# Sparse attention in a two-layer trunk: dots in three passes, the indexer's columns first, and the output product by halves of tokens

## What is computed

```python
c_q, c_kv, k_idx, w_idx = jnp.split(h @ w_in, [256, 512, 576], axis=-1)
c_q, c_kv, k_idx = rmsnorm(c_q, q_norm), rmsnorm(c_kv, kv_norm), layernorm(k_idx, kidx_g, kidx_b)
...
    q_idx = (cq_b @ w_qidx).reshape(B, Q_BLOCK, HI, DI)
    dots = jnp.einsum('bthd,bsd->btsh', q_idx, k_idx) * (DI ** -0.5)
    score = jnp.einsum('btsh,bth->bts', jax.nn.relu(dots), w_b).astype(jnp.float32)
    score = jnp.where(causal[None], score, -jnp.inf)
    _, sel = lax.top_k(score, top_k)
    ...
    q = (cq_b @ w_uq).reshape(B, Q_BLOCK, H, dh)
    p = jax.nn.softmax(logits, axis=-1)
...
return out @ w_out
```

## Time and profile before

| | us |
|---|---|
| median of 3 runs | 2018.43 |
| lowest and highest | 2018.05, 2019.6 |
| the profiled execution | 2018.26 |
| its span, first to last instruction | 2016.4 |
| TensorE busy in the span | 1980.2 (98%) |
| VectorE, ScalarE, GpSimd busy | 1346.0, 844.5, 249.7 |
| sparse attention, first to last matmul of its own | 1457.08 to 1656.80 |

### The profile page before, as it was taken

The page is one execution under the profiler, slowest core; times in us unless marked ns, Lnnn a source line. Parts: engine busy times, 40 slices in busy tenths (PEclk is TensorE's granted clock), DMA queues, the critical chain, the costliest instruction groups (busy, mean ns, idle before and its releaser), DMA issues.

```text
span 2016.4 us, 23083 instructions
## 1 busy us (share of the span) xinstructions
PE 1980.2 (98%) x9030; PEld 1618.4 (80%) x9030; DVE 1346.0 (67%) x1673; ACT 844.5 (42%) x1151; POOL 249.7 (12%) x183
## 2 busy tenths in 40 slices
PE   8999999999999999999999999999998899999997
PEld 7788888877877888888888888888875688888886
DVE  7999944443534447999843899983458658999732
ACT  5555632132222224554631555562266535555520
POOL 0000012010010141000021000002224650000031
PEclk9999999999999999999999999999999999999998
DMA  4233123312212232242131333222231013322221
GB/s 168 84 122 129 58 102 112 113 64 100 84 68 85 82 105 84 84 147 104 58 115 64 119 141 110 84 87 100 81 105 42 1 63 142 109 84 98 100 93 65
DMA packets 69719, 189.45 MB, mean 94 GB/s; under 512 B 4016, under 2 KB 12208, under 8 KB 64496
## 3 DMA queue, kind: packets, MB, share of 16 engines
q1 hardware_dynamic: 69376, 187.25, 26.5%
q0 software_dynamic: 240, 0.79, 0.1%
HBM read 185.92 MB, written 2.10 MB: 93 GB/s over the span
## 4 chain that ended last, share of the span: by engine, by line
PE 87%; DVE 6%; issue 3%; ACT 2%; POOL 1%; SPq 0%; DMA 0%; POOLq 0%; DVEq 0%; ACTq 0%
PE bank L1804 13%; PE bank L1806 13%; PE bank L1805 13%; PE bank L1812 12%; PE bank L1814 12%; PE bank L1813 12%; PE bank L1818 2%; PE bank L1820 2%; PE bank L1819 2%; PE bank L2021 2%; PE bank L1911 2%; DVE part_lo L1182 1%; PE bank L2011 1%; PE bank L2130 1%; POOL dsa_temp L712 1%
## 5 line engine op out<-in xcount | busy, mean ns | idle before, releaser
L741 ACT ACTIVATE part_hi<-quad_w 128x1024 fp32r<-128x1024 f32 x280 | 293.2, 1064 | 279.5 <-PE bank L1814 199.8
L1182 DVE TENSOR_TENSOR part_lo<-quad_w,part_hi 128x1024 fp32r<-128x1024 f32 x280 | 330.0, 1217 | 25.7 <-ACT part_hi L741 25.3
L1804 PE MATMUL bank<-gated_hi,out_hi 128*128 128x512 f32 x704 | 274.8, 390 | 0.0
L1806 PE MATMUL bank<-gated_hi,out_lo 128*128 128x512 f32 x704 | 274.1, 389 | 0.0
L1805 PE MATMUL bank<-gated_lo,out_hi 128*128 128x512 f32 x704 | 274.1, 389 | 0.0
L1812 PE MATMUL bank<-part_hi,s_hi 128*128 128x512 f32 x640 | 252.6, 395 | 2.4 <-DVE part_lo L1182 2.4
L1814 PE MATMUL bank<-part_hi,s_lo 128*128 128x512 f32 x640 | 249.6, 390 | 0.0
L1813 PE MATMUL bank<-part_lo,s_hi 128*128 128x512 f32 x640 | 249.2, 389 | 0.0
L1812 PE MATMUL bank<-part_hi,xn_hi 128*128 128x512 f32 x608 | 238.8, 393 | 4.7 <-DVE part_lo L1182 4.7
L1814 PE MATMUL bank<-part_hi,xn_lo 128*128 128x512 f32 x608 | 237.9, 391 | 0.0
L1813 PE MATMUL bank<-part_lo,xn_hi 128*128 128x512 f32 x608 | 237.7, 391 | 0.0
(11 more groups left out here) (207 smaller groups left out, 3385.8 us busy)
## 6 DMA issues: line engine op xcount, KB each, us to landing
quad_w<-w_ffn_in SPq DMA_DIRECT2D x80, 1024.0 KB, 7.3
out_raw<-w_ffn_out SPq DMA_DIRECT2D x64, 704.0 KB, 4.0
w_raw<-w_ret_in SPq DMA_DIRECT2D x24, 1024.0 KB, 4.8
rest_raw<-w_ffn_in SPq DMA_DIRECT2D x32, 256.0 KB, 5.8
w_raw<-w_ret_out SPq DMA_DIRECT2D x8, 1024.0 KB, 4.8
w_raw<-w_dsa SPq DMA_DIRECT2D x8, 1024.0 KB, 4.8
x_res<-x_in SPq DMA_DIRECT2D x8, 256.0 KB, 6.3
out<-x_res SPq DMA_DIRECT2D x8, 256.0 KB, 2.2
```

Source lines behind the costliest of these rows:

```text
L741: nc.scalar.activation(in_four(part_hi[part_slot(h)]), source, copy).then_inc(part_hi_made, 1)
L1182: nc.vector.tensor_tensor(in_four(part_lo[part_slot(h)]), source, in_four(part_hi[part_slot(h)]).bitcast(FP32), ALU.subtract)\
L1804: mm(to, w_hi_of[:, at:at + width], hi, start=start, stop=False)
L1806: return mm(to, w_lo_of[:, at:at + width], hi, start=False, stop=stop)
```

## The change

- The unit of the indexer's columns goes first, so that its product, the transposes and the layer norm of the index keys stand beside the query latents. Latents are squared and scaled from PSUM, without a copy; the key latents' product is spread, its last two pieces between the first dots. Their squares and root come after the first block's dots.
- Index queries and keys are split in high and low parts, and each dot is three passes.
- GpSimd splits the low parts of units 5 to 11; the projection of queries and two output units get buffers of their own.
- The output product is made in two halves of 256 tokens. The early half (tokens 0 to 255) is one tile d ahead of each of the steps 18 to 25 on TensorE, into bank 7, with an update on VectorE. The late half comes after the steps, in banks 0 and 1, and the low parts for the next sublayer of tiles 0 to 3 wait for tile 3.
- Rounds of the last block: 4 ahead of the steps and 12 between them, two each at steps 18, 19, 20. The results' split comes one step sooner.

```diff
-DSA_SIZES = [UNIT, CHUNKS * IDX_COLS, UNIT // 2, UNIT // 2, RANK // P * IDX_HEADS * IDX_DIM] \
+DSA_SIZES = [CHUNKS * IDX_COLS, UNIT, UNIT // 2, UNIT // 2, RANK // P * IDX_HEADS * IDX_DIM] \
...
+    dsa_out_parts = [(at(f"dsa_out_hi{n}", x_at + (1 + n) * CHUNKS * chunk, UNIT, FP32R),
+                      at(f"dsa_out_lo{n}", x_at + (1 + n) * CHUNKS * chunk + 4 * UNIT, UNIT, FP32R))
+                     for n in range(2)]
...
-    ROUND_STEPS = (8, 10, 11, 13, 14, 16, 17, 18, 19, 20)
-    EARLY_ROUNDS = TOP_K // 8 - len(ROUND_STEPS)
-    POOL_SPLITS = (DSA_UNITS - DSA_OUT_UNITS - 2, DSA_UNITS - DSA_OUT_UNITS + 2)
+    ROUNDS_AT = {8: 1, 10: 1, 12: 1, 14: 1, 16: 1, 17: 1, 18: 2, 19: 2, 20: 2}
+    EARLY_ROUNDS = TOP_K // 8 - sum(ROUNDS_AT.values())
+    CHOICE_STEP = max(ROUNDS_AT) + 1
+    EARLY_OUT = 18
+    POOL_SPLITS = (DSA_UNITS - DSA_OUT_UNITS - 2, DSA_UNITS)
...
+        if SUBLAYERS[s] == "dsa" and u - FIRST_UNIT[s] == 5:
+            return w_raw[u % 2], uq_hi, uq_lo
+        n = u - FIRST_UNIT[s] - (DSA_UNITS - DSA_OUT_UNITS)
+        if SUBLAYERS[s] == "dsa" and 0 <= n < 2:
+            return (w_raw[u % 2],) + dsa_out_parts[n]
         return w_raw[u % 2], w_hi[u % 2], w_lo[u % 2]
...
+        return cols(bank[2 * part + b // 2], b % 2, RANK)
...
-        return bank[5 + q % 3]
+        return bank[5 + q % 2]
+    def early_out():
+        return bank[7][:, :HALF_SEQ]
+    def late_out(d):
+        return bank[d % 2][:, :HALF_SEQ]
...
+                inverse_rms_3(0, 1)
+                inverse_rms_3(1, 0)
+                split_unit(u0 + 5)
+                inverse_rms_3(2, 2)
+                pool.wait_ge(r_col3_done, 3)
+                nc.gpsimd.tensor_tensor(r_col3[:, 2 * BLOCKS:], r_col3[:, 2 * BLOCKS:], r_col[:, :], ALU.mult)\
+                    .then_inc(r_col3_done, 1)
...
                 split_unit(u0 + POOL_SPLITS[0] + 2)
+                split_unit(u0 + POOL_SPLITS[0] + 3)
                 for i in range(VECTOR_STEPS, len(STEPS)):
+                    if i == 2 * HEADS - 4:
+                        split_unit(u0 + POOL_SPLITS[0] + 4)
+                    elif i == 2 * HEADS:
+                        split_unit(u0 + POOL_SPLITS[0] + 5)
                     _, _, probs, _, _, at = step_bufs(i)
                     pool.wait_ge(inverted, i + 1)
                     nc.gpsimd.tensor_scalar(probs, probs, row_inv[:, at], None, ALU.mult)\
                         .then_inc(pool_probs_done, 1)
-                split_unit(u0 + POOL_SPLITS[0] + 3)
...
+            if SUBLAYERS[stage_of(u)] == "dsa" and n >= DSA_UNITS - DSA_OUT_UNITS:
+                act.wait_ge(unit_done, u - 3)
+            elif n >= 2 and SUBLAYERS[stage_of(u)] != "ffn" and (SUBLAYERS[stage_of(u)], n) != ("dsa", 5):
...
+                act.wait_ge(unit_done, u0 + 5)
+                square_latents(1)
+                act.wait_ge(r_col3_done, 4)
...
-                    if i == HEADS:
-                        split_unit(u0 + 9)
+                    if i in (2, 6, 10):
+                        split_unit(u0 + DSA_UNITS - DSA_OUT_UNITS + 1 + i // 4)
                     copy_probs_t(i)
                     if i + 2 < len(STEPS):
                         exps(i + 2)
-                    if i % 4 == 1 and i > 4:
+                    if i % 4 == 0 and i >= 4:
                         result_hi(i // 4 - 1)
                 result_hi(len(STEPS) // 4 - 1)
+                act.wait_ge(unit_done, u0 + DSA_UNITS - DSA_OUT_UNITS + 1)
...
+                dve.wait_ge(latents_squared, 2 * BLOCKS)
+                mean_squares(2, RANK)
...
+                    if i % 4 == 1 and i > 4:
+                        result_lo(i // 4 - 1)
+                    for n in range(ROUNDS_AT[i] if i in ROUNDS_AT else 0):
+                        if n > 0:
+                            mark_8(last_block)
                         find_8(last_block)
-                    elif i == ROUND_STEPS[-1] + 1:
+                    if i == CHOICE_STEP:
                         choice_to_bias(last_block)
-                    if i % 4 == 2 and i > 4:
-                        result_lo(i // 4 - 1)
+                    if 0 <= i - EARLY_OUT < CHUNKS:
+                        early_update(i - EARLY_OUT)
                 result_lo(len(STEPS) // 4 - 1)
-                dve.wait_ge(w_lo_made, u0 + POOL_SPLITS[1])
+                dve.wait_ge(w_lo_made, u0 + DSA_UNITS)
                 for d in range(CHUNKS):
                     u = u0 + DSA_UNITS - DSA_OUT_UNITS + d // 2
                     if d == CHUNKS - 1:
...
                         dve.wait_ge(half_done, 2 * RET_HEADS + d // 2 + 1)
                     else:
                         dve.wait_ge(unit_done, u + 1)
-                    update(s, d, 4 + d % 2, 1.0)
-                    if d % 2 == 1 and d // 2 + 2 < DSA_OUT_UNITS:
-                        split_unit(u + 2)
-                    stream_lo(s + 1, d)
+                    late_update(d)
+                    if d == 3:
+                        for e in range(4):
+                            stream_lo(s + 1, e)
+                    elif d > 3:
+                        stream_lo(s + 1, d)
...
+                    to = bank[DOT_BANKS[c % 4]][:, :keys]
+                    mm(to, q_idx_hi[rows, queries], k_idx_hi[rows, :keys], start=True, stop=False)
+                    mm(to, q_idx_hi[rows, queries], k_idx_lo[rows, :keys], start=False, stop=False)
+                    mm(to, q_idx_lo[rows, queries], k_idx_hi[rows, :keys], start=False, stop=True)\
+                        .then_inc(dots_done, 1)
                 for c in range(IDX_HEADS):
+                    if c == 4:
+                        key_latents(6)
+                    if c == 6:
+                        key_latents(7).then_inc(unit_done, 2)
...
+                def out_products(to, d, tokens, ks):
+                    u = u0 + DSA_UNITS - DSA_OUT_UNITS + d // 2
+                    pe.wait_ge(w_lo_made, u + 1)
+                    for k in ks:
+                        done = product(to, None, (d % 2 * HEADS + k) * P, cols(o_hi, k)[:, tokens],
+                                       cols(o_lo, k)[:, tokens], k == 0, k == HEADS - 1,
+                                       of=unit_bufs(u)[1:])
+                    return done
+                early, late = slice(0, HALF_SEQ), slice(HALF_SEQ, SEQ)
                 for i in range(len(STEPS)):
+                    d = i - EARLY_OUT
+                    if 0 <= d < CHUNKS:
+                        if d == 0:
+                            pe.wait_ge(o_lo_made, 4)
+                        else:
+                            pe.wait_ge(early_updated, d)
+                        out_products(early_out(), d, early, range(HEADS)).then_inc(early_out_done, 1)
                     turn_probs(i)
                     if i + 3 < len(STEPS):
                         logits(i + 3)
                     if i >= 1:
                         results(i - 1)
                 results(len(STEPS) - 1)
+                pe.wait_ge(o_lo_made, 7)
+                for d in range(2):
+                    out_products(late_out(d), d, late, range(HEADS // 2))
+                pe.wait_ge(o_lo_made, 8)
                 for d in range(CHUNKS):
-                    u = u0 + DSA_UNITS - DSA_OUT_UNITS + d // 2
-                    if d % 2 == 0:
-                        pe.wait_ge(w_lo_made, u + 1)
                     if d >= 2:
                         pe.wait_ge(x_updated, CHUNKS * s + d - 1)
-                    for k in range(HEADS):
-                        if d == 0:
-                            pe.wait_ge(o_lo_made, len(STEPS) // 4 - 1 + k // 4)
-                        done = product(bank[4 + d % 2][:, :], u % 2, (d % 2 * HEADS + k) * P,
-                                       cols(o_hi, k), cols(o_lo, k), k == 0, k == HEADS - 1)
-                    done.then_inc(unit_done if d % 2 else half_done, 1)
+                    ks = range(HEADS // 2, HEADS) if d < 2 else range(HEADS)
+                    out_products(late_out(d), d, late, ks).then_inc(unit_done if d % 2 else half_done, 1)
```

More of the change, by code:

```diff
@@ L487, in latent_bank, with latent_columns @@
         return bank[(5, 6, 2, 3)[n]]
+    def latent_columns(part, b):
+        return cols(bank[2 * part + b // 2], b % 2, RANK)
     def scores_of(b):
@@ L2059, in latent_products @@
                     for b in range(BLOCKS):
-                        done = product_by_token(
-                            bank[b][:, part * RANK:(part + 1) * RANK], tile(xn_hi, k * BLOCKS + b),
-                            tile(xn_lo, k * BLOCKS + b), slot, at, RANK, k == 0, k == CHUNKS - 1)
+                        done = product_by_token(latent_columns(part, b), tile(xn_hi, k * BLOCKS + b),
+                                                tile(xn_lo, k * BLOCKS + b), slot, at, RANK,
+                                                k == 0 and b % 2 == 0, k == CHUNKS - 1 and b % 2 == 1)
                     return done
@@ new lines, in _ @@
```

(9 more changed lines are left out.)

178 lines of the change are left out of this document (88 added, 90 removed).

## The result

| | before | after |
|---|---|---|
| median, us (4 runs each) | 2018.24 | 2035.03 |
| lowest and highest | 2018.04, 2019.6 | 2033.98, 2041.2 |
| the profiled execution | 2018.26 | 2033.99 |

The ratio is 1.0087, 95% interval 1.0072 to 1.0101: slower, as forecast (2035.0), and close to the forecast in size. The terms behind it are another matter, and the rows are read for them. The same five stretches as in the earlier trace rows, in the kernel after the change (length, busy us of PE, PEld, DVE, ACT, POOL, PE clock, DMA): steps 0 to 7, steps 8 to 15, steps 18 to 25, steps 26 to the last, then the output product up to the next layer's first matmul.

A forecast was written before the change was run, and what follows sets the result against it. The top-128 search sets when the steps start; a chain over GpSimd, ScalarE and VectorE paces them up to step 18. Terms -3.0 + 4.9 + 1.4 + 7.8 - 0.5 + 1.5 + 22.3 - 1.2 - 20.5 + 4.0 = +16.7: 2035.0 us (2021 to 2043).

The forecast's parts named there:

- start of step 0: First of 32 attention steps, one per query block and head: starts 3.0 us earlier (from -4.6 to -1).
- steps 0 to 7 (lock, ScalarE at 6): VectorE's step 4 scaling waits for GpSimd's split behind ScalarE's: +4.9 us; another ScalarE split at step 6: +1.4.
- steps 8 to 15 (GpSimd at 12 and 16): GpSimd's 4.6 us low parts stand ahead of its scalings of steps 12 and 16: +3.8 and +4.0 us.
- steps 16 to 25 (early half): Eight early-half output tiles, 23.0 us, ahead of the transposes of steps 18 to 25, filling 1.5 us: +22.3 us.
- end: Last output tiles to next feed-forward layer: GpSimd's sums and VectorE's low parts delay its first part, +4.0 us (0 to 6).
- rounds and clock, spread: Six instead of seven search rounds ahead of step 18, -0.5 us; half clock behind TensorE's holes, +1.5 (0 to 4).
- Rival A: VectorE's scaling and bias go through beside GpSimd: +1.5 instead of +4.9 us, total 2029; chance 0.17.
- a dot so costs 1.07: Dots of 384 keys between projections: 1.07 us each before, three passes about 0.52, so TensorE gains some 0.5 on each of 16.
- the second block's scores come some 0.7 us earlier: Ahead of the search's second block: faster dots bring its scores 0.7 us earlier, taking back the first mask's +0.8.
- no more than 1 us either way: Ahead of the projections and dots: the same products only change places, at most 1 us gained or lost.
- the middle bias: VectorE's bias of the second block, at 1541.7, falls into GpSimd's 4.6 us split and waits to 1543.3.
- they fill the 1.5 us of holes there: Steps 18 to 25: the early half's tiles fill TensorE's 1.5 us of free time.

The follow-up runs named there:

- run 1: Changed kernel with GpSimd's low parts of the last two output units ahead of its scalings of steps 21 and 23 instead of 12 and 16: 2026.14 us.
- run 2: On run 1: GpSimd's low part of the second output unit moved to step 19, ScalarE's high part of the last unit from step 10 to 22: 2023.22 us.
- run 3: On run 2: ScalarE's high parts at steps 17, 19 and 22 instead of 2, 6 and 22: 2019.03 us (1.0005).
- run 11: On run 10: the last 16 dots stand in pairs between the projections: 2011.68 us (0.9962).
- run 8: On run 3: VectorE's low parts behind output tiles one tile later, the next layer's first part ahead of tile 6's update instead of 7's: 2014.78 us.
- run 4: On run 3: the early half's eight tiles behind step 31 instead of ahead of steps 18 to 25, splits left where they were: 2042.3 us.
- run 7: On run 3: GpSimd squares and sums only 32 of 512 columns of the tiles behind the attention sublayer: 2015.76 us.
- run 13: On run 8: early half behind step 31 on two alternating banks, ScalarE's last three splits at 28, 30 and after, GpSimd's behind all its scalings: 2023.9 us.
- run 10: On run 8: key latents turned behind projection 3 instead of 1, ScalarE's weight split earlier, its latent scaling behind copies of projections 0 and 1: 2011.53 us.

## Why the prediction was right, and where only its sum was

| stretch | predicted | in the two profiles |
|---|---|---|
| start of step 0 | -3.0 | -2.10 |
| steps 0 to 7 (lock, ScalarE at 6) | +6.3 | +5.78 |
| steps 8 to 15 (GpSimd at 12 and 16) | +7.8 | +8.11 |
| steps 16 to 25 (early half) | +22.3 | +21.08 |
| steps 26 to 31 and last results | -1.2 | -0.64 |
| late half | -20.5 | -19.98 |
| end | +4.0 | +3.10 |
| rounds and clock, spread | +1.0 | in the rows above |
| sum | +16.7 | +15.35 |

Of the start, 0.37 us come from ahead of the sublayer, whose first matmul is at 1456.71 instead of 1457.08. Of the end, 2.58 us lie between the last tile and the next layer's first matmul, and 0.52 behind it. The medians differ by 16.8, since the changed kernel's executions spread upwards from the profiled one.

**The splits: right, in place, size and cause.** The waits at steps 12 and 16 were forecast at about 4 us each and are 3.97 and 4.18, and the scaling of step 4 came where the prediction had it, with a wait of 4.01. Runs 1 and 2 took these waits away, the last down to 0.41, by moving the splits that were said to cause them (run 2 moved ScalarE's of step 10 too, to no effect). ScalarE's splits at steps 2 and 6 were put at 1.5 and 1.4, and run 3 won 2.2 us between steps 0 and 18 without them, so they cost somewhat less. The rule of the Trainium skill, page "SBUF — State Buffer", section "SBUF: two separate sides", that of a GpSimd operation and a VectorE operation in a two-port mode or with two SBUF inputs the later one fully blocks, agrees with the 3.88 us row, if the scaling ran in such a mode, which no run shows. Rival A (no lock) is out for the scaling. Not every operation is locked out: between 1571.42 and 1575.93, under a split of GpSimd, a search round's maximum (0.69) and replacement (0.68) took what they always take.

**The start: three errors, of which two cancel in part.** First, "a dot so costs 1.07" took the whole of what is left beside six matmuls for the dot itself, and set three passes of 0.174 against it. The rows after show 0.92 a dot of 384 keys: three passes, 0.16 apart, are 0.48, and some 0.45 stands beside them, as it does at 512 keys. What was saved is 0.14 us a dot, not 0.5. TensorE did not reach step 0 six us early but 0.7 late (1550.97 instead of 1550.30), and waited 1.28 us there instead of 4.05. Since the search sets the start, this did not count in the sum. Second, "the second block's scores come some 0.7 us earlier" and "no more than 1 us either way" missed a wait that the new order makes: ScalarE gets to the key latents late, TensorE stands still for 1.11 and 1.19 us, the clock falls, and the scores are 2.06 us late. (GpSimd's first addition of these scores is as late, 2.05 us, behind a split that waited 2.65 us for ScalarE; how much each chain adds is not shown.) Third, the middle bias was to be locked out for 1.6 us; it slipped by 0.17 us ahead of GpSimd's split (0.41 us long) and the wait did not come. Run 11 shows how near that was: 1.10 us. The start was -2.1 by luck as much as by reasoning.

**The clock: right in kind, one place missed.** I allowed 1.5 us in all for half clock behind the holes. In steps 0 to 15 the mean clock was 0.77 and 0.84, where it had been 0.81 and 1.00. What that cost by itself no run shows; the splits, the round and the clock together were put at 15.1 us (6.3 + 7.8 + 1.0), and the two stretches grew by 13.9. I did not see that a shorter hole in the middle of the projections can do it too, for a time that is not the same in each profile (last section). The changed kernel spreads over 7 us where the one before spreads over 1.6; that this comes from the half clock near 1503 is likely, and not shown.

**The product: right in sum, wrong in what it hides.** The product did cost 1.1 us more than it saved (+21.08 - 19.98; 1.8 forecast). But "they fill the 1.5 us of holes there" counts only the holes of the old kernel. The runs show 6.9 us hidden in steps 18 to 25 and 9.1 in the whole time. Most of the difference is in the rounds: steps 18 to 20 have six where they had three, 4.5 us more. Had I costed these at the steps that receive them and then let the product hide them, the sum would have been much the same, and it would have been plain that the filler pays for the earlier start. (The prediction's "15.72 / 9" divides eight steps by nine; with 15.72 / 8 a step is 5.0 us on TensorE, not 4.8, still above VectorE's 4.2.) What stays true is that the steps with the large holes, 0 to 15, are out of its reach.

**The end: right in its main part.** The contention and the late first part were named; 4.0 against 3.10. The wait of 1.8 us at tile 6 did not come: TensorE waited 0.2 us for VectorE's updates. That the end needed only another order (run 8) was not seen.

## What to carry to other kernels

Cost a piece of work by the step that receives it, not by its length: the same 4.6 us on GpSimd cost 4 us at steps 12 and 16 and nothing at steps 21 and 23. When a filler is added, move the work that needs cover under it in the same edit; here that turned +0.87% into +0.05% (run 3), and the orders, the pairs and the rounds of the later runs made -0.46% of it. And before a difference of two rows is called the price of an instruction, ask what else lies between them: the 0.45 us beside each dot did not shrink with its passes.

## What the hardware showed unexpectedly

- How long TensorE stays at half clock behind the same holes is not fixed. Behind the same two waits of 1.11 and 1.19 us near 1503 the rows show no half clock in four profiles (runs 3, 4, 7 and 13), about 3.5 us in two (the kernel after and run 8), 7 in run 1 and nearly 17 in run 2, with TensorE busy for 15.49 of 16 us in it:

```profile
1504.00:1520.00 16.00, 15.49 (x34) 10.04 (x35) 9.76 (x30) 8.32 (x17) 7.55 (x4) 0.50 0.20 67
```

  The steps then started at 1550.91 (run 3) or 1558.47 (run 2). What decides it is open. Run 3 spread over 8.2 us and run 10, without these waits, over 1.8; but run 8 kept them and spread over 1.9.
- Two 64-row dots back to back, on rows 0 to 63 and 64 to 127, cost clearly less than two apart (1.95 instead of 2.48 us each, with six 128-row matmuls counted to each), and their passes run two at a time, 0.23 us for both (run 11).
